# First attention: the scores of two steps side by side on TensorE

## The reference

```python
qkv = h @ w_qkv[l]
qa, ka, va, qb, kb, vb = jnp.split(qkv, QKV_SPLITS, axis=-1)
# heads 0-7: norm and axial rope of q and k, then
s = jnp.einsum('bqkgd,bskd->bkgqs', qi, k, ...) * scale   # 2 k/v heads
p = jax.nn.softmax(s, axis=-1)
o = jnp.einsum('bkgqs,bskd->bqkgd', p, v, ...)
# heads 8-15: rope, then a mixture of three dilated windows; the sum of
# exponentials over three patterns with a common maximum and denominator
heads = jnp.concatenate([out_a, out_b], axis=-1)
x = x + _rmsnorm(heads @ w_out[l], mix_post_g[l])
```

## Time and profile before

| | |
|---|---|
| median of 3 runs | 2075.71 us |
| profiled execution, device time | 2075.74 us |
| its span, first to last instruction | 2073.6 us |
| around the span | 2.14 us |
| TensorE busy | 2057.8 us, 99% |
| VectorE, ScalarE, GpSimd busy | 37%, 39%, 44% |
| TensorE, mean granted clock | 1.000 |
| TensorE in the chain that ended last | 94% |

### The profile page before, as it was taken

One profiled execution on the slowest core, in us unless ns is written; L12 is line 12 of the kernel. 1 busy time (PEld: TensorE's weight loads), 2 busy tenths in 40 slices (PEclk: granted clock), 3 DMA queues, 4 the chain that ended last, 5 costly groups with the idle time before them and its releaser, 6 DMA issues.

```text
span 2073.6 us, 24499 instructions
## 1 busy us (share of the span) xinstructions
PE 2057.8 (99%) x9914; PEld 1695.8 (82%) x9914; DVE 777.3 (37%) x1302; ACT 807.2 (39%) x1420; POOL 916.9 (44%) x468
## 2 busy tenths in 40 slices
PE   9999999999999999999999999999999999999998
PEld 8888888877788888888888887888888788888887
DVE  3111100777844111100356674711132676562112
ACT  4222322467754222212534543522234445352222
POOL 4444444246662444444434443544434443264442
PEclk9999999999999999999999999999999999999999
DMA  6333323221033333223322222333233222223331
GB/s 186 99 97 96 99 95 112 78 73 41 31 102 102 102 92 101 92 101 101 117 89 75 72 82 71 103 100 95 99 114 105 72 73 80 82 92 100 93 101 71
DMA packets 244256, 191.26 MB, mean 92 GB/s; under 512 B 6448, under 2 KB 208816, under 8 KB 243760
## 3 DMA queue, kind: packets, MB, share of 16 engines
q1 hardware_dynamic: 244144, 189.70, 29.5%
HBM read 187.58 MB, written 2.10 MB: 91 GB/s over the span
## 4 chain that ended last, share of the span: by engine, by line
PE 94%; DVE 3%; ACT 1%; issue 1%; SPq 0%; DMA 0%; POOL 0%; DVEq 0%; ACTq 0%
PE bank L1666 29%; PE bank L1668 28%; PE bank L1667 28%; PE bank L1660 3%; PE bank L1889 1%; PE bank L2057 1%; PE bank L1909 1%; PE bank L1916 1%; DVE xn L1145 0%; DVE x_tok L1150 0%; PE bank L2086 0%; PE bank L2088 0%; DVE m_sum L1640 0%; DVE br_lo L1541 0%; DVE xn L1174 0%
## 5 line engine op out<-in xcount | busy, mean ns | idle before, releaser
L628 POOL TENSOR_TENSOR w_lo<-w_raw,w_hi 128x1024 fp32r<-128x1024 f32 x326 | 789.3, 2431 | 875.9 <-ACT w_hi L716 875.2
L1666 PE MATMUL bank<-xt_hi,w_hi 128*128 128x512 f32 (+1 forms) x1504 | 579.4, 385 | 0.9 <-POOL w_lo L628 0.5
L1667 PE MATMUL bank<-xt_lo,w_hi 128*128 128x512 f32 (+1 forms) x1504 | 575.4, 383 | 0.0
L1668 PE MATMUL bank<-xt_hi,w_lo 128*128 128x512 f32 (+1 forms) x1504 | 575.4, 383 | 0.0
L716 ACT ACTIVATE w_hi<-w_raw 128x1024 fp32r<-128x1024 f32 x326 | 341.9, 1054 | 243.5 <-DMA w_raw<-in_ffn_w_down 142.6
L1666 PEld LDWEIGHTS bank<-xt_hi,w_hi 128*128 128x128 f32 x1504 | 282.7, 188 | 63.4 <-issue 6.7
L1668 PEld LDWEIGHTS bank<-xt_hi,w_lo 128*128 128x128 f32 x1504 | 282.7, 188 | 55.3
L1667 PEld LDWEIGHTS bank<-xt_lo,w_hi 128*128 128x128 f32 x1504 | 282.8, 188 | 53.5
L1244 DVE TENSOR_TENSOR h_raw<-bank,act_gate 128x512 f32<-128x512 f32 x44 | 30.4, 692 | 400.1 <-PE bank L1668 400.1
L1666 PE MATMUL bank<-w_hi,xt_hi 128*128 128x512 f32 (+1 forms) x456 | 178.2, 391 | 0.0
L1668 PE MATMUL bank<-w_hi,xt_lo 128*128 128x512 f32 (+1 forms) x456 | 174.4, 383 | 0.0
(11 more groups left out here) (298 smaller groups left out, 2851.0 us busy)
## 6 DMA issues: line engine op xcount, KB each, us to landing
w_raw<-in_w_in SPq DMA_DIRECT2D x132, 512.0 KB, 3.7
w_raw<-in_ffn_w_down SPq DMA_DIRECT2D x44, 512.0 KB, 3.5
w_raw<-in_ffn_w_gate SPq DMA_DIRECT2D x43, 512.0 KB, 3.7
w_raw<-in_ffn_w_up SPq DMA_DIRECT2D x43, 512.0 KB, 3.8
w_raw<-in_w_out SPq DMA_DIRECT2D x24, 512.0 KB, 3.5
w_raw<-in_w_branch SPq DMA_DIRECT2D x24, 512.0 KB, 3.3
w_raw<-in_w_qkv SPq DMA_DIRECT2D x16, 512.0 KB, 3.7
x_tok<-in_x SPq DMA_DIRECT2D x4, 512.0 KB, 7.0
```

What stands on the lines that cost most here:

```text
L628: pool.tensor_tensor(lo_slots[i], raw_slots[i], f32(hi_slots[i]), ALU.subtract).then_inc(lo_ready, 1)
L1666: pe.matmul(out_ap, ah, bh, start=first, stop=False)
L1667: pe.matmul(out_ap, ah, bl, start=False, stop=False)
L1668: return pe.matmul(out_ap, al, bh, start=False, stop=last)
```

## The change

TensorE's loop issues no scores in even steps. In an odd step k, behind the transposes of step k (and the first half of a unit, where one is due), it issues `scores(k + 2)` and `scores(k + 3)` one behind the other.

```diff
                 if k % 3 == 0 and 0 < k // 3 < UNITS:
                     unit_half(k // 3, 0)
-                if k + 3 < STEPS:
-                    scores(k + 3)
+                if k % 2 == 1:
+                    for j in (k + 2, k + 3):
+                        if j < STEPS:
+                            scores(j)
                 if k % 3 == 1 and 0 < k // 3 < UNITS:
                     unit_half(k // 3, 1)
                 if k % 2 == 0 and k >= 2:
```

## The result

The changed kernel takes 2105.69 us, the median of 4 runs (2101.98 to 2109.67), against 2075.7 us (2075.49 to 2075.71). The ratio is 1.0145, 95% interval 1.0133 to 1.0157: slower by 30 us. The forecast was 2100.5 us in a range from 2091 to 2109. The profiled execution has a span of 2102.2 us, 28.6 more than before.

A forecast was written before the change was run, and what follows sets the result against it. TensorE, busy 99% of the span, was taken as the bound. To the 2073.6 us span came 14.2 us up to step 23's transposes and 10.6 at the end: 2098.4, with 2.14 around it 2100.5 us, range 2091 to 2109.

The forecast's parts named there:

- The chain: From the start of the scores to the next step's transposes: 3.22 us, and 3.49 us from step 16 on.
- Point 1: Steps 3, 9, 15, 21, nothing behind the scores: next transposes late by 1.93 us twice and 2.20 twice, sum 8.3 us.
- Point 2: Steps 5, 11, 17, a swap behind the scores: 2.2 us lost twice, 2.5 in step 17, sum 6.9 us.
- Point 3: Steps 7, 13, 19: half a unit covers the chain, no loss; swaps of following even steps late, sum 1.1 us.
- Point 4: Step 1: transposes of step 3 start at 457.4 rather than 456.91, with the second head late, 0.6 us.
- Point 5: Joining two score blocks saves 0.27 us a pair; ten pairs up to the transposes of step 23, -2.7 us.
- Point 6: The end, transposes of step 23 to those of 30, without unit work: 34.8 us instead of 24.2, +10.6 us.
- The sign change: VectorE's small instruction in the chain, exposed to the port lock with GpSimd: up to 1.2 us more per wait, taken as free.
- the clock: Rival: TensorE, about 70% busy in the last 34 us, runs them at 1.2 GHz: 2125 us, chance 3%.
- the joined blocks pay and the waits are covered: Rival: 14 joins at 0.22 to 0.42 us make it 3 to 6 us faster, 2070 to 2073 us, chance 3%.
- Only the end pays: Rival: waits where units are come out near nothing; 8 us, up to 14, slower: 2084 to 2090 us, chance 12%.
- Even steps pay too: Rival: odd steps' own transposes wait for the second maximum, ten steps pay 1 us more: 2108 to 2112 us, chance 10%.

The follow-up runs named there:

- e11: Changed kernel with the first half of the unit in steps 3, 9, 15 and 21 put behind the two score blocks: 2095.41 us, ratio 1.0095.
- e3: Kernel before with scores issued in pairs in steps 7, 13 and 19 only: 2074.34 us against 2075.63, ratio 0.9993.
- e5: Changed kernel plus 12, 12 and 18 idle transposes ahead of the transposes of steps 26, 28 and 30: 2101.75 us, ratio 1.0128.
- e10: Kernel before with seven joined score pairs beside half units, in steps 3, 7, 9, 13, 15, 19 and 21: 2073.7 us against 2075.68, ratio 0.999.
- e4: Changed kernel with score pairs only up to step 21, TensorE's old order from step 22: 2093.02 us, ratio 1.008.
- e8: Changed kernel with VectorE's reciprocal, `unit_cos` and low part ahead of the next maximum, `out_sum` in odd turns: 2109.15 us, ratio 1.0158.
- e9: Same VectorE order as e8, but with TensorE's order of the kernel before: 2112.99 us, ratio 1.0182.
- e7: Changed kernel with only the reciprocal of step k+1 put ahead of the maximum of step k+2 on VectorE: 2112.64 us, ratio 1.0175.

## Why the prediction was right, and where it was not

**The chain, right.** Scores to the next transposes: 3.21 us in step 3 (forecast 3.22) and 532.16 - 528.65 = 3.51 in step 15 (3.49). These two rows of the changed kernel were

```profile
528.65 1.66 PE L1889 MATMUL bank<-unit_hilo,unit_hilo 64*128 64x512 f32 x12
532.16 1.32 PE L1660 MATMUL bank<-ident,probs 128*128 128x128 f32 x8 [1.85 <-POOL probs L651]
```

**Point 1, right.** Four waits of 1.55, 1.55, 1.85 and 1.85 us; e11 took away just these.

**Point 2, right.** Swap waits of 1.95, 1.95 and 2.23 us; the transposes of step 6 start 4.29 us behind the scores (forecast 4.21).

**Point 3, right in kind.** Steps 7, 13 and 19 have no wait. The swaps of steps 14 and 20 waited 0.22 and 0.32 us, not 0.5 and 0.6.

**Point 4, right.** The transposes of step 3 start at 457.42, forecast 457.4.

**Point 5, the saving, sized too small.** I took 0.27 us for a join. Behind a matmul it is 0.43 (e3): 0.09 on the way in, 0.22 in the block, and the way out, which I had left aside. TensorE in e3, a single block and the matmuls behind it:

```profile
462.76 0.96 PE L1889 MATMUL bank<-ka_hilo,qa_hilo 64*128 64x512 f32 x6
463.65 0.50 PE L1666 MATMUL bank<-xt_hi,w_hi 128*128 128x512 f32 x1
463.99 0.39 PE L1667 MATMUL bank<-xt_lo,w_hi 128*128 128x512 f32 x1
464.22 0.39 PE L1668 MATMUL bank<-xt_hi,w_lo 128*128 128x512 f32 x1
```

The first matmul is followed after 0.34 us, the second after 0.23: 0.11 us for the way out. So a block on its own costs 0.42 us more than one that joins another. The Trainium skill (TensorEngine Tiling (Array Packing), Key Properties) says that a change of tiling mode drains TensorE. The trace agrees that there is a gap on both sides of a block, 0.09 and 0.11 us; that it is a drain no row shows.

**Point 6, right.** 34.48 us at full clock (e5), forecast 34.5 to 34.8.

**The sign change, rightly left at its free value.** The prediction allowed 1.2 us more for line 1357 in each chain. In the changed kernel its 16 instructions took 0.17 us at the median and 0.47 at most.

Of the 28.6 us between the two spans, 14.5 lie ahead of the transposes of step 23 (572.27 against 557.73; forecast 14.2), 11.5 between them and those of step 30, and the last 2.6 behind those.

**What the sum lacked is the clock.** I had it as a rival, all or nothing, at 2125 us and 3%. It fell, but only in places: a mean of 0.94 over 30 us from 500 and of 0.83 over 30 us from 590 is (0.06 + 0.17) x 30 x 2 = 14 us at the lower level in the profiled execution. What that cost there:

- Behind the transposes of step 30, 2.2 of the 2.6 us (e5 needs only 0.4 more than the kernel before).
- Between the transposes of 23 and 30, 35.65 - 34.48 = 1.2 us.
- Of the 14.5 us, 1.2 to 1.5. The same work takes 5.82 us from the transposes of step 6 to those of step 7 and 7.01 us from those of 12 to those of 13, at the low clock. And e5, whose profiled run had one more such stretch ahead of step 23, reached it 1.48 us later.

That makes some 5 us of clock and leaves some 24 us of waits less joins, against my 24.8. So the profiled execution lies 3.8 us above the forecast though the waits less joins were a little less than forecast, and the median of the four runs is 1.4 us higher still. The range held the median, but in part by luck: its upper part was there for longer waits, nothing in it stood for the clock, and the longest run, 2109.67 us, lies outside it.

Of the other rivals, "the joined blocks pay and the waits are covered" holds only where something covers them (e3, e10). "Only the end pays" fell with e4. "Even steps pay too" did not happen: the transposes of the odd steps, which follow the second maximum, show no wait from step 3 on.

**What stays open.** No experiment took the wait away by VectorE's order without bringing another one. That the queue holds the reciprocal is shown by the trace (input ready at 457.01, start at 463.64), and that cover removes the wait is shown by e11, e3 and e10; what the time would be with a queue that hides both the exponential and the late scores, no run shows. What the 3.8 us between e8 and e9 are made of was not taken apart. Nor was what decides in which execution the clock falls.

## What to carry to other kernels

- Before moving work later on the bound engine, look not only for who waits for it, but for what is queued behind those who wait. Here the step that paid was not the one whose scores came late but the one before it, whose reciprocal stood behind them in VectorE's queue.
- Such a move cost nothing where the bound engine had other work as long as the chain, 3.2 to 3.5 us here. Make it in those places only: three and seven joins gained 1.3 and 2.0 us where fourteen lost 30.
- A queue order that looks careless can be what hides a latency. The reciprocal behind the next maximum hid the exponential. With the reciprocal alone in front, VectorE waited 10.7 us for it (e7); with `unit_cos` and the low part in front as well, 36 us, and that kernel was 37 us slower under TensorE's old order (e9).

## What was not expected of the hardware

The granted clock fell to 0.50 behind waits of which none was over 2.54 us. From 504 to 508 us TensorE was busy for 2.05 us of 4; from 508 on it was at the 1.2 GHz level. The same stretch of step 5, with the same wait of 1.95 us, kept 1.00 in the profiled run of the changed kernel, but in that of e5 it was followed by 0.50:

```profile
476.00:478.00 2.00, 2.00 (x10) 1.90 (x9) 1.99 (x5) 0.96 (x2) 1.20 (x1) 0.50 0.00 0
```

It cost about 5 us in the profiled execution of the changed kernel. Its runs lie between 2101.98 and 2109.67 us, where all runs of the kernel before lie within 0.51 us (2075.39 to 2075.90). With 42 idle transposes in the waits of the end the clock stayed at 1.00 there, which was worth 3.4 us between the two profiled executions.
